# Block-product FFN: eight products in its first two steps, seven in the others, and the second convolution step behind the down additions

## The reference, cut to what matters

```python
def _conv_ffn(h, w_up, conv_w, conv_b, w_down):
    z = h @ w_up.astype(h.dtype)
    u, v = z[..., :D_FF], z[..., D_FF:]                  # D_FF = 3072
    u = _dwconv(u, conv_w, conv_b, (1, 1))               # width 3 over positions
    return (jax.nn.gelu(u) * v) @ w_down.astype(h.dtype)

f_lat = _conv_ffn(_modulate(_rms_norm(x, norm_pre_ffn[i]), sh_f, sc_f), ffn_w_up[i], ...)
x = x + g_f * _rms_norm(f_lat, norm_post_ffn[i])
```

## Time and profile before

| What | Value |
|---|---|
| Median of 3 runs | 2282.79 us (2282.76 to 2282.83) |
| The profiled execution | 2283.22 us, span 2281.5 us |
| Mean granted TensorE clock of that execution | 0.956 |
| TensorE busy | 2086.4 us (91%) |
| VectorE busy | 1565.5 us (69%) |
| ScalarE busy | 809.9 us (35%) |
| GpSimd busy | 1343.6 us (59%) |

### The profile page before, as it was taken

How to read it: one execution, slowest core, us unless ns; L and a number is a source line. 1 busy time by engine, 2 the same in 40 slices (tenths; PEclk the granted TensorE clock), 3 DMA queues, 4 the chain that set the end, 5 groups by cost and what they waited for, 6 DMA issues and landing times.

```text
span 2281.5 us, 26751 instructions
## 1 busy us (share of the span) xinstructions
PE 2086.4 (91%) x9040; PEld 1677.3 (74%) x9040; DVE 1565.5 (69%) x1535; ACT 809.9 (35%) x1072; POOL 1343.6 (59%) x836
## 2 busy tenths in 40 slices
PE   7899997976799999999999969668999999999996
PEld 7677775765677777777777758656888888888885
DVE  6688987078577777777777684786555666655567
ACT  3567575245122222323222335442322222232222
POOL 1423233357577877777777643465766666776663
PEclk9999998978899999999999979779999999999998
DMA  6232231221122222222222320101111111111114
GB/s 268 70 115 87 93 111 36 107 111 41 55 83 86 70 92 83 83 75 81 83 83 90 122 74 19 74 28 46 46 55 46 55 55 55 46 46 55 46 46 148
DMA packets 52120, 174.91 MB, mean 77 GB/s; under 512 B 4817, under 2 KB 5105, under 8 KB 50929
## 3 DMA queue, kind: packets, MB, share of 16 engines
q1 hardware_dynamic: 52080, 174.41, 22.1%
HBM read 161.80 MB, written 12.58 MB: 76 GB/s over the span
## 4 chain that ended last, share of the span: by engine, by line
PE 67%; DVE 15%; ACT 8%; issue 7%; POOL 2%; ACTq 0%; DVEq 0%; DMA 0%; POOLq 0%
PE ps L713 32%; PE ps L462 26%; PE ps L594 3%; DVE S L1847 2%; PE ps L825 1%; ACT S L1059 1%; DVE V L1451 1%; DVE Y L1758 1%; PE ps L501 1%; DVE T_lo L1841 1%; ACT TH L988 1%; DVE Y L1538 1%; PE ps L537 1%; DVE T_raw L1807 1%; PE ps L792 1%
## 5 line engine op out<-in xcount | busy, mean ns | idle before, releaser
L1758 DVE TENSOR_TENSOR Y<-Y,ps 128x1024 f32<-128x1024 f32 x336 | 393.3, 1213 | 14.1 <-PE ps L462 2.2
L1361 POOL TENSOR_TENSOR F_lo<-S,F_hi 128x1024 fp32r<-128x1024 f32 x42 | 101.2, 2409 | 314.4 <-ACT F_hi L1101 314.4
L462 PE MATMUL ps<-F_hi,WC_hi 128*128 128x512 f32 x736 | 239.9, 404 | 44.0 <-DVE Y L1758 22.7
L1342 POOL TENSOR_TENSOR So_lo<-So_raw,So_hi 128x512 fp32r<-128x512 f32 x138 | 238.4, 1755 | 2.2 <-ACT So_hi L886 2.2
L462 PE MATMUL ps<-F_hi,WC_lo 128*128 128x512 f32 x736 | 232.2, 393 | 0.0
L462 PE MATMUL ps<-F_lo,WC_hi 128*128 128x512 f32 x704 | 220.5, 395 | 0.0
L886 ACT ACTIVATE So_hi<-So_raw 128x512 fp32r<-128x512 f32 x138 | 83.8, 624 | 369.7 <-POOL So_raw L1256 369.7
L462 PEld LDWEIGHTS ps<-F_hi,WC_hi 128*128 128x128 f32 x736 | 136.2, 191 | 90.6 <-DVE Y L1758 39.5
L1101 ACT ACTIVATE F_hi<-S 128x1024 fp32r<-128x1024 f32 x44 | 46.7, 1061 | 435.9 <-DVE S L1865 435.9
L1891 DVE TENSOR_TENSOR U<-t,ps 128x512 f32<-128x512 f32 x46 | 31.6, 687 | 225.2 <-PE ps L713 225.2
L462 PEld LDWEIGHTS ps<-F_hi,WC_lo 128*128 128x128 f32 x736 | 139.9, 190 | 30.4
(11 more groups left out here) (271 smaller groups left out, 5324.1 us busy)
## 6 DMA issues: line engine op xcount, KB each, us to landing
rawA<-wA SPq DMA_DIRECT2D x60, 512.0 KB, 3.3
rawB<-wB SPq DMA_DIRECT2D x60, 512.0 KB, 3.3
E<-ada SPq DMA_DIRECT2D x47, 512.0 KB, 3.3
rawC<-wC SPq DMA_DIRECT2D x46, 512.0 KB, 3.3
quad<-ada SPq DMA_DIRECT2D x8, 2048.0 KB, 9.2
ada_first<-ada SPq DMA_DIRECT2D x4, 2048.0 KB, 16.3
outT<-X SPq DMA_DIRECT2D x16, 512.0 KB, 2.8
X<-outT SPq DMA_DIRECT2D x16, 512.0 KB, 6.9
```

Source lines behind the costliest of these rows:

```text
L462: mm = pe.matmul(out, w[:, w_cols:w_cols + P], (hi, lo)[part], start=first and w is W_hi[s] and part == 0, stop=last and w is W_lo[s])
L1342: TT(lo[:, at:at + HF], src, hi[:, at:at + HF].bitcast(F32), ALU.subtract).then_inc(op_ready, 1)
L1361: TT((F_lo_last if last else F_lo)[:], S[1][:], F_hi[:].bitcast(F32), ALU.subtract)\
L1758: TT(Y[:, m], Y[:, m], flat(ps[:, b:b + 2, :]), ALU.add).then_inc(d_added, 1)
```

## The change

Steps 0 and 1 of each layer's FFN become plain steps (eight products each); steps 2 to 23 stay block steps with seven. `step_at(L, j)` counts the block steps, `UP` is now 22, and `DN` (23) counts the down products of a layer. What moves with it:

- TensorE: the unit of step 1 for u stands first, then in layer 0 the count product and the first ada columns, then `down(L, 0)` with three pairs of banks instead of two, then the unit for v, then step 2. The first copy of product 11 waits for the fourth `T_lo`.
- ScalarE and GpSimd: step 1's weights are rounded whole. The combinations are made for step 2, behind the remainder of the first F, and no longer in the stream before the FFN. The rounding and remainder of layer 1's first down weights move from before that stream into the FFN. `T_raw`'s fourth block lies in `V` and `acc1`.
- VectorE: the convolution of step 1 stands behind the eight copies of `down(L, 0)`, ahead of the remainders of T2 and T3. In every block step but the last the second convolution step moves from ahead of the eight down additions to behind them, at the start of the next `ffn_step`, ahead of a reduction and of `gated`. GeLU's place in ScalarE's order and the order of SyncE's `ffn_loads` are as before; `load_up(L, 2)` waits for the whole remainders, and the first E loads stand between the first weight loads.

The diff, cut to its core:

```diff
-UP = FJ - 1
+UP, DN = FJ - 2, FJ - 1
...
+        def step_at(L, j):
+            return UP * L + (j - 1)
...
             def ffn(L):
                 save_x(2 * L)
+                if L == 0:
+                    load_unit(2)
                 load_up(L, 2)
-                ffn_loads(L, 1)
+                if L == 0:
+                    load_unit(3)
+                load_up(L, 3)
                 with sp_.Fori(2, FJ - 2) as j:
...
             # TensorE, ffn(L)
-                ffn_step(L, 1)
-                with pe.Fori(2, FJ - 1) as j:
+                unit("A", N_STD + 2 * L + 1, AB23)
+                if L == 0:
+                    pe.wait_ge(u_evac, 1)
+                    pe.wait_ge(cols_full, 16)
+                    pe.matmul(ps[:, 0, 8:8 + 4 * KT], cnt_row[0:4 * KT], ident[0:4 * KT, 0:4 * KT],
+                              start=True, stop=True).then_inc(cols_made, 1)
+                    ada_columns(4 * NH + 2, 2, ps[:, 0, 0:2])
+                down(L, 0)
+                pe.wait_ge(d_added, 8 * FJ * L + 6)
+                unit("B", N_STD + 2 * L + 1, AB01)
+                ffn_step(L, 2)
+                with pe.Fori(3, FJ - 1) as j:
...
             # ScalarE, ffn_first(L)
+                round_second("A", L)
+                copy_u(L, 0, AB01)
+                round_second("B", L)
                 if L:
-                    act.wait_ge(conv_done, FJ)
...
+                    round_down(L, 0)
                 round_t(L, 0)
+                round_t(L, 2)
                 gelu(L, 0)
                 round_t(L, 1)
+                round_f(L, 0)
+                copy_u(L, 1, AB23)
+                for name in ("S4", "S1", "11", "12", "S2"):
+                    round_op(name, L, 2)
+                gelu(L, 1)
+                for s in "AB":
+                    act.wait_ge(unit_done[s], N_STD + 2 * L + 2)
                 round_t(L, 3)
+                for name in ("S3", "22"):
+                    round_op(name, L, 2)
...
             # GpSimd, ahead of layer 1's stream, in the stream, and ffn_first(L)
-            lo_of_unit("C", UP)
             next_stream(5, 2, lambda h: fill_ffn(1, h))
...
-                    for name in MADE_ORDER:
-                        combine(name, q // 4, 1)
                     lo(1)
...
+                lo_of_unit("A", N_STD + 2 * L + 1)
+                lo_of_unit("B", N_STD + 2 * L + 1)
+                if L:
+                    lo_of_unit("C", DN * L)
+                else:
+                    ada_product(2)
+                f_remainder(L, 0)
+                for name in MADE_ORDER:
+                    combine(name, L, 2)
+                for name in READY_FIRST[:5]:
+                    lo_of_op(name, L, 2)
+                if L == 0:
+                    ada_product(3)
...
             # VectorE
             def ffn_first(L):
                 right_raws(L)
+                if L == 0:
+                    dve.wait_ge(cols_made, 1)
+                    dve.wait_ge(ada_out, NH + 2)
+                    dve.reciprocal(cc[:, 1], ps[:, 0, 8:8 + 4 * KT]).then_inc(cols_step, 1)
+                    add_ada_bias(ps[:, 0, 0:2], 48, 2, NH + 2)
                 right_lo(L, 0)
+                if L == 0:
+                    ada_sum(1, 0)
                 add_down(L, 0)
+                taps(L, 1)
                 right_lo(L, 1)
                 right_lo(L, 2)
...
                 if not first:
-                    if L == 0:
-                        ada_sum(j - 1, 1)
-                    gated(L, j - 1)
+                    conv_right(L, j - 1)
+                if L == 0:
+                    ada_sum(j - 1, 1)
+                gated(L, j - 1)
...
-                taps(L, j, v_first_half)
+                conv_left(L, j)
+                dve.wait_ge(op_done, done_at("22", t))
+                TT(V[:, hs(0)], U2[:], p["22"], ALU.subtract).then_inc(up_added, 1)
                 if not last:
                     add_down(L, j - 1)
                     return
+                conv_right(L, j)
```

More of the change, by code:

```diff
@@ L411, in ffn_loads @@
             def ffn_loads(L, j):
-                if not (isinstance(j, int) and j == 1):
-                    load_down(L, j - 1)
+                load_down(L, j - 1)
                 if L == 0:
@@ L718, in ffn_step @@
             def ffn_step(L, j):
-                t, c = UP * L + j, FJ * L + j
+                t, c = step_at(L, j), FJ * L + j
                 static = isinstance(j, int)
-                first, last = static and j == 1, static and j == FJ - 1
+                first, last = static and j == 2, static and j == FJ - 1
                 if not (first and L == 0):
@@ L726, in ffn_step @@
                 quarter("12", t, first)
-                if not first:
-                    if L == 0:
[L729 to L732, removed]
+                pe.wait_ge(d_added, 8 * (c - 1))
+                if L == 0:
+                    if first:
+                        pe.wait_ge(f_mul, 2)
+                    pe.wait_ge(ada_added, NH + j)
+                    ada_columns(4 * NH + 2 * j, 2, ps[:, 0, 0:2])
                 quarter("S4", t, first)
-                if first:
-                    down(L, 0)
                 quarter("S1", t, first)
@@ L742, in ffn_step @@
                 quarter("22", t, first)
[L743 to L749, removed]
+                if not last:
                     down(L, j - 1)
@@ L1097, in ffn_step @@
                 static = isinstance(j, int)
-                first, last = static and j == 1, static and j == FJ - 1
-                if not first:
-                    act.wait_ge(f_mul, t)
-                    A(F_hi[:], S[1][:], ACT.Copy).then_inc(f_hi, 1)
-                    copy_p1(t)
-                    round_down(L, j - 1)
+                last = static and j == FJ - 1
+                round_f(L, j - 1)
+                copy_p1(t)
+                round_down(L, j - 1)
                 if not last:
@@ L1131, in ffn @@
                 ffn_first(L)
-                ffn_step(L, 1)
-                with act.Fori(2, FJ - 1) as j:
+                ffn_step(L, 2)
+                with act.Fori(3, FJ - 1) as j:
                     ffn_step(L, j)
@@ L1355, in ffn_step @@
             def ffn_step(L, j):
-                t = UP * L + j
                 static = isinstance(j, int)
-                first, last = static and j == 1, static and j == FJ - 1
-                if not first:
-                    pool.wait_ge(f_hi, t)
-                    TT((F_lo_last if last else F_lo)[:], S[1][:], F_hi[:].bitcast(F32), ALU.subtract)\
-                        .then_inc(f_ready, 1)
+                last = static and j == FJ - 1
+                f_remainder(L, j - 1, F_lo_last if last else F_lo)
@@ L1363, in ffn_step @@
                 if L == 0:
                     ada_product(2 * j)
-                if not first:
-                    lo_of_unit("C", t - 1)
+                lo_of_unit("C", DN * L + (j - 1))
                 if last:
@@ L1753, in add_down @@
                     dve.wait_ge(d_done, 8 * (FJ * L + j) + m + 1)
-                    b = (4, 0)[m % 2] if isinstance(j, int) and j == 0 else (4, 0, 6)[m % 3]
+                    b = (6, 4, 0)[m % 3] if isinstance(j, int) and j == 0 else (4, 0, 6)[m % 3]
                     if isinstance(j, int) and j == 0:
@@ L1874, in ffn_step @@
             def ffn_step(L, j):
-                t = UP * L + j
+                t = step_at(L, j)
                 static = isinstance(j, int)
-                first, last = static and j == 1, static and j == FJ - 1
+                first, last = static and j == 2, static and j == FJ - 1
                 p = {name: ps[:, OUT[name]] for name in OPS}
@@ L1886, in ffn_step @@
                 TT(u_0, t1[:], p["12"], ALU.add).then_inc(up_added, 1)
-                if L == 0 and not first:
+                if L == 0:
                     add_ada_bias(ps[:, 0, 0:2], 46 + 2 * j, 2, NH + 1 + j)
```

178 lines of the change are left out of this document (92 added, 86 removed).

## The result

| What | Before | After |
|---|---|---|
| Median | 2282.78 us (4 runs) | 2302.99 us (2302.49 to 2303.39, 4 runs) |
| The profiled execution | 2283.22 us, span 2281.5 us | 2302.49 us, span 2300.8 us |
| Mean granted clock | 0.956 | 0.959 |
| U2 of step 2, layer 0, starts | 620.05 | 601.17 |
| Mean of the 21 periods to step 23 | 32.19 us | 33.94 us |

A forecast was written before the change was run, and what follows sets the result against it. TensorE was taken to bound layer 1's loop (unbroken chain) and nearly fill layer 0's, with waits at FFN entries. Terms -2.0 - 3.5 - 17.8 - 15.2 + 11.6 + 1.5 = -25.4 gave 2257.8, median 2257 us; range 2222 to 2274.

The forecast's parts named there:

- Stream and beginnings: Work ahead of the FFNs: gains 2.0 (1.0 per layer) and 3.5 in layer 1; FFN entries: 17.8 and 15.2 us.
- the tail of layer 0: After layer 0's step 23, where U2 is late too: the tail ends some 1.5 us later.
- Rival C: FFN entries: VectorE's work stays, so the wait only moves to the second unit; half the gain, 2274 us; chance 0.09.
- cost and gain nil: Layer 1's loop, convolution step behind the additions: dependents 7 to 10 us later, TensorE already unbroken, period stays 30.75 us.
- The sign that the prediction gave for this case: Layer 1's loop: a period longer than 30.75 us would mean the late down weights had become a bound.
- the ring of 32.6: Layer 0's loop from U2 through additions, moved step, GeLU, rounding, rawB and E: 32.6 us a step, +11.6 us.
- The 6.97: Layer 0's loop: time in us from U2 to the down additions, without the moved convolution step.
- its largest doubt: Layer 0's loop: when E's load lands; 1 us there is 21 us in the time.
- B: Layer 0's loop above 33.8 us makes the kernel slower; at 34.6, with E later, 2299 us; chance 0.06.
- A1: Layer 0's loop: E lands early enough, TensorE sets the pace, a step gains 0.85 us; 2226 us; chance 0.15.
- The Trainium skill's figures: Layer 0's loads: three in 6.4 us after first issue, a step of about 31.4 instead of 32.6, 2231 us.
- TensorE's own time: TensorE's need per loop step: 30.75 us in layer 1 (48 down products 11.15, 84 up products 19.60), 31.2 in layer 0.

The follow-up runs named there:

- e1: Changed kernel with the second convolution step moved back ahead of the down additions, the plain steps kept: 2247.05 us, ratio 0.9847.
- e4: Changed kernel with ScalarE rounding S1 of the next step behind the convolution's middle tap instead of ahead of it: 2225.81 us, ratio 0.9754.
- e5: Changed kernel with the down weights' load rawC issued ahead of rawB on SyncE's queue: 2227.32 us, ratio 0.9760.
- e3: Changed kernel with ScalarE rounding 22 of the next step ahead of the GeLU: 2217.44 us, ratio 0.9719.
- e9: Changed kernel with rawC and each step's first E load issued ahead of rawB on SyncE's queue: 2209.15 us, ratio 0.9680.
- e6: Changed kernel with ScalarE rounding 22 ahead of the GeLU and S1 behind the middle tap: 2212.48 us, ratio 0.9694.
- e7: Kernel before with the second convolution step behind the additions and 22 rounded ahead of the GeLU: 2248.07 us, ratio 0.9854.

## Why the prediction was wrong

*Stream and beginnings: the mechanism right, their sum 2.8 us too good.* Layer 0 was to gain 17.8 and half of the stream's 2.0; U2 of step 2 starts 18.9 earlier. Layer 1 was to gain 15.2, 1.0 and 3.5, less 1.5 for the tail of layer 0, 18.2 in all; the stretch between the loops is 15.3 shorter. The single marks were off both ways. From the first unit to step 3 it is 617.74 - 539.27 = 78.5 us in layer 0 (forecast 82) and 1599.33 - 1521.99 = 77.3 in layer 1 (forecast 72). In layer 0 tile 3 came at 562.35 (565.0 forecast, a stand of 2.78 us instead of 4) and rawB was issued at 590.69 (595.5), so that U2 started at 601.17 (607.0); E's load behind rawB set it, as foreseen. That 18.9 agrees with 17.8 + 1.0 is in part luck: the forecast gain was that of step 3's start, and at U2 its marks gave 620.05 - 607.0 = 13. In layer 1 the down products of step 2 started 61.7 us after the unit (forecast 61), but TensorE then stood 2.89 us before tile 3: the first convolution step had waited for S1's rounding, the detour that holds the loop. Rival C is out: e1 gains 36.0.

*Layer 1, "cost and gain nil": the step that failed first, 16.7 us.* The forecast asked only when the down weights are needed by TensorE, and there it was right: their remainder is done at 1900.27, 4.1 us before TensorE starts on them at 1904.39 (4.5 forecast). It named everything that comes 7 to 10 us later, rawC among it, and did not follow rawC to its next user in each engine's own order: GpSimd's remainder of the down weights, and behind it the combination of S1, and in ScalarE's order S1's rounding ahead of the tap. e4 and e5 show this: each takes away one link, e4 without touching any load, and each brings layer 1 to 30.51. The sign that the prediction gave for this case, a longer period by late down weights as a bound, saw the right load but not the way it acts.

*Layer 0, the ring of 32.6: the mechanism was half right, its size wrong, +36.8 where +11.6 was said.* By its terms, in the step shown: second step to rawB 897.52 - 893.22 = 4.30, forecast 1.6 + 1.61 + 1.4 = 4.61; rawB to U2 11.02, forecast 11.5; U2 to the additions 8.45, forecast 6.97; the additions to the next second step 928.11 - 916.99 = 11.12, forecast 9.62. As means of the 20 whole rounds of the loop they are 4.30, 11.30, 8.45 and 9.94. The first two are good. The third is the term that was mis-sized: 8.45 in every round with the detour over S1, 5.75 without it (e4). The 6.97 was read from a step in which S1's rounding happened to be done 0.36 us before the tap could start (848.42 + 0.63 against 849.41), and the detour was already to be seen in rows 6's own step of the kernel before, from which the link of 11.47 was taken:

```profile
624.25 0.63 ACT L886 ACTIVATE So_hi<-So_raw 128x512 fp32r<-128x512 f32 x1 [7.16 <-POOL So_raw L1256]
624.78 1.23 ACT L1059 ACTIVATE S<-Ub,par 128x1024 f32<-128x1024 f32 x1
626.17 1.84 DVE L1847 SCALAR_TENSOR_TENSOR S<-Ub,par,S 128x1024 f32<-128x1024 f32 x1 [2.59 <-ACT S L1059]
```

There the additions begin at 630.13, 10.08 us after U2 (620.05), and without the 1.61 of the second convolution step between them that is 8.47. Both numbers read from this one step would have given a ring of about 34.1. The fourth term is 9.54 in the 15 rounds without slow pairs and 11.14 in the five with them, where the additions wait for TensorE. So the loop was not too long because E landed late, which the prediction named as its largest doubt: that link came out 0.2 us shorter than forecast.

*Rivals.* B named the same ring and the right sign, at a chance of 0.06, but priced a slower E and the moved step at 2.32; the moved step took 1.28 and E's link was shorter than forecast. Its threshold, a loop of 33.8, was met by way of S1; that its 2299 lies near the measured 2303 is luck, since it had layer 1 unchanged. A1 would have needed a cut: e3 and e9 are A1, with a step of 30.9. The Trainium skill's figures ("DMA: Bandwidth & Descriptors", sections Specifications and Anatomy of one DMA) would have three loads in 6.4 us after the first issue. The 2.0 us stand there in a section of the Trainium skill on transfers that GpSimd issues, while SyncE issues these. Here GpSimd's product starts 904.66 - 897.52 = 7.14 us after it, between those and the 7.6 of rows 6. The difference is not what decided.

*TensorE's own time was taken too long.* Rows 3 were read as 48 products without a wait. A row of the waits in layer 1's steps, of the kernel before, shows that there is one (total us, times, longest), and the pairs at tile 3 show how small it is (start, us):

```profile
PEld ps L462 <- DVE Y L1758: 7.5, 20, 0.4
```

```profile
1650.18 0.61 PE L462 MATMUL ps<-F_hi,WC_lo 128*128 128x512 f32 x2
1650.75 0.73 PE L462 MATMUL ps<-F_hi,WC_hi 128*128 128x512 f32 x2
```

The weight load, not the product, waits 0.4 us in each step for the addition; pairs otherwise start 0.45 to 0.46 us apart, here 0.57, and the first takes 0.73. So the moved step had a gain to give in layer 1 as well: 30.8 us a step before, 30.51 in e4, e5, e6, e7 and e9, some 0.3 x 21 = 6 us.

*What stays open.* In layer 0 the periods of the changed kernel vary from 32.8 to 35.8 us. The five with slow pairs take 35.2 us as a mean and the other 16 take 33.5, so the slow pairs make up some 8.5 of the 36.8 us (5 x 1.7); why they follow five of 21 stands of nearly the same length is not shown. e5's layer 0 (31.74) shows that E alone, behind rawB, still sets the pace; e4's 31.51 was not tried with E's load moved.

## What to carry to other kernels

Before an operation is moved behind another, follow what waits for it once round, through every in-order stream it passes (each engine's program and the DMA queue), until the ring comes back to the operation itself or leaves; the sum of that ring, with the work now inside it (here the 9.62 us of additions), is the new lower bound of a step, whatever TensorE's load. A ring that is held by orders and not by data is cheap to cut: two swapped lines were worth 85.6 us. And a link's duration is only good for the state in which it was read: take all links of a ring from one step, and one in which the loads are as late as they will be (here step 2 of the kernel before), since in rows 4's step the detour over S1 was hidden by 0.36 us.

## What the runs showed of the hardware

Of loads that are issued close together the later ones take longer to land. In the kernel before each kind of 512 KB load took 3.3 us as a median. In the changed kernel rawB, which goes first, took 3.4; in layer 0's steps rawC behind it took 5.2, and the first E behind both took 5.5 in the step shown, while the second E of that step, issued alone at 908.8, took 3.3. In layer 1, with rawB and rawC alone, rawC took 4.6. It is the place and not the kind: in e9's layer 0, where rawC goes first and rawB last, rawC took 3.2 and rawB 4.5.

In the step shown a stand of TensorE of 1.79 us before tile 3 was followed by a mean granted clock of 0.60 over the next 4.3 us (most of them at the lower level, 1.2 GHz), though TensorE was busy for 4.05 of them; before and after it was 1.00, the upper level. But in 16 of the 21 steps a stand of 1.5 to 1.9 us at the same place was followed by no slow pair, so its length alone does not decide it:

```profile
909.00:918.00 9.00, 7.46 (x32) 5.55 (x30) 6.26 (x8) 2.66 (x4) 8.84 (x7) 1.00 0.19 58
918.00:922.30 4.30, 4.05 (x11) 3.18 (x12) 3.68 (x4) 0.78 (x2) 4.30 (x4) 0.60 0.38 122
922.30:930.00 7.70, 7.70 (x35) 6.32 (x34) 6.69 (x6) 0.58 (x1) 2.14 (x2) 1.00 0.00 0
```

The columns are the length, the busy time of PE, PEld, DVE, ACT and POOL, the granted clock, the DMA share and GB/s, of the changed kernel. Pairs of products take up to 1.05 us there, against 0.62 at 1.00. The five slow pairs run from 918.25 to 922.23, 3.98 us, where five pairs 0.455 us apart need 2.28: the wait of 1.79 us cost another 1.7 in slow products.
